# Two ways through the branch, gated sums by halves and a reordered second routing in a kernel of two transformer blocks

## What is computed

```python
def second_block(x, c, ...):
    cond = silu(c)
    for i in range(2):
        sh1, sc1, g1, sh2, sc2, g2 = split(cond @ ada_w[i] + ada_b[i], 6)
        h = modulate(rmsnorm(x, norm_g[i, 0]), sh1, sc1)
        y = mla_mixer(h, ...) if i == 0 else mamba2_mixer(h, ...)
        x = x + g1 * y
        h = modulate(rmsnorm(x, norm_g[i, 1]), sh2, sc2)
        y = swiglu(h, ...) if i == 0 else moe_swiglu(h, ...)
        x = x + g2 * y
    return rmsnorm(x, final_norm)

def moe_swiglu(h, w_router, w_gate, w_up, w_down):      # 8 experts, 2816 hidden features
    top_vals, top_idx = top_k(t @ w_router, 2)
    gates = sum(one_hot(top_idx, 8) * softmax(top_vals)[..., None], axis=1)
    for e in range(8):
        out = out + gates[:, e:e + 1] * swiglu(t, w_gate[e], w_up[e], w_down[e])
```

## Time and profile before

| | us |
|---|---|
| median of the runs | 2639.09 |
| profiled execution | 2639.72 |
| its span | 2638.0 |
| TensorE busy | 2205.1 (84%) |
| VectorE busy | 1437.7 (55%) |
| ScalarE busy | 1154.7 (44%) |
| GpSimd busy | 38.4 (1%) |
| DMA queue q1, share of the span | 66.9% |

### The profile page before, as it was taken

One profiled execution on the slowest core, in us unless ns is written; L12 is line 12 of the kernel. 1 busy time (PEld: TensorE's weight loads), 2 busy tenths in 40 slices (PEclk: granted clock), 3 DMA queues, 4 the chain that ended last, 5 costly groups with the idle time before them and its releaser, 6 DMA issues.

```text
span 2638.0 us, 29032 instructions
## 1 busy us (share of the span) xinstructions
PE 2205.1 (84%) x11922; PEld 1648.2 (62%) x11922; DVE 1437.7 (55%) x1992; ACT 1154.7 (44%) x1488; POOL 38.4 (1%) x107
## 2 busy tenths in 40 slices
PE   6888798766666665788899788877999999999997
PEld 6767566641122211456798677666887887878875
DVE  4744434442101100332554566655989988988997
ACT  3432334310000000242344356634777777777775
POOL 0000100000000000000000000000000000000000
PEclk9889898878777888897899889887999999999999
DMA  7441830329999999566345332143989989989994
GB/s 254 173 179 49 295 120 32 115 107 409 409 409 409 409 409 409 179 237 242 128 143 196 126 128 96 64 168 116 342 321 369 336 320 369 338 319 370 337 337 190
DMA packets 267673, 656.66 MB, mean 249 GB/s; under 512 B 13439, under 2 KB 38531, under 8 KB 267529
## 3 DMA queue, kind: packets, MB, share of 16 engines
q1 hardware_dynamic: 266576, 652.90, 66.9%
q10 hardware_dynamic: 952, 1.77, 0.2%
HBM read 653.60 MB, written 1.05 MB: 248 GB/s over the span
## 4 chain that ended last, share of the span: by engine, by line
PE 67%; DMA 16%; DVE 9%; ACT 5%; issue 2%; POOL 0%; ACTq 0%; DVEq 0%; POOLq 0%
PE psum L241 16%; PE psum L242 16%; PE psum L243 16%; PE psum L236 11%; DMA ring<-in_w_expert_up 5%; DMA ring<-in_w_expert_down 5%; DMA ring<-in_w_expert_gate 5%; PE psum L2257 2%; PE psum L1029 2%; PE psum L821 1%; DVE w_lo L186 1%; ACT w_hi L176 1%; PE psum L2279 1%; DMA ring<-in_ada_w 1%; PE psum L1975 1%
## 5 line engine op out<-in xcount | busy, mean ns | idle before, releaser
L186 DVE TENSOR_TENSOR w_lo<-ring,w_hi 128x1024 fp32r<-128x1024 f32 (+1 forms) x778 | 904.9, 1178 | 412.1 <-ACT w_hi L176 398.9
L176 ACT CAST w_hi<-ring 128x1024 fp32r<-128x1024 f32 (+1 forms) x778 | 785.1, 1015 | 437.7 <-PE psum L243 433.9
L241 PE MATMUL psum<-w_hi,xg_hi 128*128 128x512 f32 (+1 forms) x768 | 294.1, 383 | 1.2 <-ACT xg_lo L1947 1.2
L243 PE MATMUL psum<-w_lo,xg_hi 128*128 128x512 f32 (+1 forms) x768 | 289.1, 376 | 0.0
L242 PE MATMUL psum<-w_hi,xg_lo 128*128 128x512 f32 (+1 forms) x768 | 288.9, 376 | 0.0
L2257 PE MATMUL psum<-ring,hT 128*32 128x512 f32 x1024 | 166.4, 785 | 124.1 <-DMA ring<-in_w_expert_gate 63.7
L2257 PEld LDWEIGHTS psum<-ring,hT 128*32 128x32 f32 x1024 | 32.2, 128 | 252.8 <-DMA ring<-in_w_expert_up 92.4
L2116 DVE TENSOR_TENSOR x<-x,psum 128x1024 f32<-128x1024 f32 x16 | 19.5, 1222 | 267.5 <-PE psum L236 267.5
L241 PEld LDWEIGHTS psum<-w_hi,xg_hi 128*128 128x128 f32 x768 | 144.7, 188 | 30.4 <-issue 1.8
L242 PEld LDWEIGHTS psum<-w_hi,xg_lo 128*128 128x128 f32 x768 | 144.7, 188 | 29.0 <-issue 1.7
L243 PEld LDWEIGHTS psum<-w_lo,xg_hi 128*128 128x128 f32 x768 | 144.5, 188 | 28.5
(11 more groups left out here) (651 smaller groups left out, 3794.5 us busy)
## 6 DMA issues: line engine op xcount, KB each, us to landing
ring<-in_moe_w_gate SPq DMA_DIRECT2D x40, 2048.0 KB, 9.1
ring<-in_moe_w_up SPq DMA_DIRECT2D x40, 2048.0 KB, 10.0
ring<-in_moe_w_down SPq DMA_DIRECT2D x40, 2048.0 KB, 9.3
ring<-in_w_expert_gate SPq DMA_DIRECT2D x32, 2048.0 KB, 16.9
ring<-in_w_expert_up SPq DMA_DIRECT2D x32, 2048.0 KB, 17.1
ring<-in_w_expert_down SPq DMA_DIRECT2D x32, 2048.0 KB, 17.9
ring<-in_ada_w SPq DMA_DIRECT2D x24, 2048.0 KB, 8.2
ring<-in_ssm_w_in SPq DMA_DIRECT2D x10, 2048.0 KB, 7.9
```

The costliest lines, as they stand in the source:

```text
L176: a.copy(self.buffers(n, src.shape)[0], src).then_inc(*self.hi_made.up())
L186: v.tensor_tensor(lo, src, hi.bitcast(F32), SUB).then_inc(*self.lo_made.up())
L241: p.matmul(o, l[0], r[0], start=start, stop=False)
L243: return p.matmul(o, l[0], r[1], start=False, stop=stop)
```

## The change

- **By halves.** A new `by_halves_pe` takes all parts of a unit first, does half 0 of the columns for all of them, signals `half`, and then does half 1, signalling each part as used. The last units of ffn's down product and of ssm_out use it. VectorE adds half 0 after `half` and half 1 after the last part.
- **Low parts.** Behind the gated sums go the last low parts of the next stage: one of four in mla, two in ffn (of the first parts of ssm) and two in ssm_out. The first of them stands behind the norm's mean, the second of a pair behind VectorE's scaling (`beside`).
- **Branch of moe1.** VectorE's last two scatter sums move into both ways of the branch: ahead of the surplus cases, or in the `Else`, as `scatter_alone`.
- **Second routing.** The table moves behind expert 0's `selg`; the Exp goes ahead of the two row copies, with a first Exp on constants, right behind the scaling; the memset of `total` waits for hT.
- **Output.** Each tile of 128 tokens is stored by a DMA of its own.

```diff
+    def by_halves_pe(p, u, h, outs, done, first, kt, k_first=0):
+
+        parts = [split.take(p, n) for n in range(split.first[u], split.end(u))]
+        for half, out_ in enumerate(outs):
+            for n, (hi, lo) in enumerate(parts):
+                for t in range(NT):
+                    w = out_[t].shape[-1]
+                    ins = split_product(p, out_[t], tiles(h, first + n - k_first, slice(t * P, (t + 1) * P)),
+                                        tuple(b[:, 0, half * w:half * w + w] for b in (hi, lo)), first + n == 0, first + n == kt - 1)
+                if half:
+                    ins.then_inc(*split.used.up())
+            if not half:
+                ins.then_inc(*done.up("half"))
...
             v.tensor_scalar(M.selg[:, t, :], slots, M.pos[:, t, bass.ds(e, 1)], M.gate[:, t, bass.ds(e, 1)],
                             ALU.is_equal, MUL).then_inc(*d.up("selg", i))
+        after_selection()
...
-            expert_dve(v, run, i, i, slots, after_gate)
+            expert_dve(v, run, i, i, slots, after_gate, nothing if i else lambda: table_dve(v, run.st, run.moe))
...
         count = e.value_load(M.tab[0:1, 0:1], min_val=0, max_val=M.most_over)
         with e.If(count > 0):
+            if first:
+                first()
             finished(e, run.st)
...
         with e.Else():
-            e.nop()
+            if alone:
+                alone()
+            else:
+                e.nop()
...
-        scatter_dve(v, run1, last)
-        over_dve(v, run1, over1)
+
+        def scatter_alone():
+            for t in range(NT):
+                v.wait_ge(*S["moe1"].pe.of("scattered", last, t))
+                v.wait_ge(*S["moe1"].dve.of("acc", last - 1, t))
+                v.tensor_tensor(x[:, t, :], x[:, t, :], banks.of("moe1", "scatter", last, t), ADD).then_inc(S["moe1"].dve.sem, 1)
+
+        over_dve(v, run1, over1, lambda: scatter_dve(v, run1, last), scatter_alone)
...
-            split.make_lo(v, min(split.end(u) + PARTS, cap))
+            split.make_lo(v, split.end(u) + PARTS - half)
...
-            by_token_pe(p, unit["ff", 2, c], mid_ff, outs, first=4 * c, kt=22)
+            if c < len(ff_chunks) - 1:
+                by_token_pe(p, unit["ff", 2, c], mid_ff, outs, first=4 * c, kt=22)
+            else:
+                by_halves_pe(p, unit["ff", 2, c], mid_ff, outs, st.pe, 4 * c, 22)
...
         norm_mean_dve(v, st, xn_ff, ss_ff)
+        split.make_lo(v, split.first[unit["ff", 0, 0]] + PARTS)
         norm_dve(v, st, xn_ff, ss_ff, modulated_gain(1), modulated_shift(1), h_ff)
...
-        for c in range(len(ff_chunks)):
-            split.make_lo(v, min(split.end(unit["ff", 2, c]) + PARTS, cap))
-        v.wait_ge(*split.multiplied(unit["ff", 2, len(ff_chunks) - 1]))
+        last = unit["ff", 2, len(ff_chunks) - 1]
+        for c in range(len(ff_chunks) - 1):
+            split.make_lo(v, split.end(unit["ff", 2, c]) + PARTS)
         for half in range(2):
+            if half:
+                v.wait_ge(*split.multiplied(last))
+            else:
+                v.wait_ge(*st.pe.of("half"))
             gated_add(v, st, half, 1, halves_of(banks.of("ff_down", half)), sil_ff[:, :, 0:512]).then_inc(*d.up("x"))
...
-        norm_dve(v, st, xn_ssm, ss_ssm, modulated_gain(0), modulated_shift(0), h_ssm)
+        split.make_lo(v, split.first[b] + 3)
+        norm_dve(v, st, xn_ssm, ss_ssm, modulated_gain(0), modulated_shift(0), h_ssm,
+                 beside=lambda: split.make_lo(v, split.first[b] + 4))
...
-            by_token_pe(p, unit["ssm_out", n], zT_parts[n], outs, first=4 * n, kt=16, k_first=4 * n)
+            if n < 3:
+                by_token_pe(p, unit["ssm_out", n], zT_parts[n], outs, first=4 * n, kt=16, k_first=4 * n)
+            else:
+                by_halves_pe(p, unit["ssm_out", n], zT_parts[n], outs, st.pe, 4 * n, 16, k_first=4 * n)
...
-        split.make_lo(v, split_ends[1] + PARTS)
-        v.wait_ge(*split.multiplied(unit["ssm_out", 3]))
+        split.make_lo(v, split_ends[1])
         for half in range(2):
+            if half:
+                split.make_lo(v, split_ends[1] + 2)
+                v.wait_ge(*split.multiplied(unit["ssm_out", 3]))
+            else:
+                v.wait_ge(*st.pe.of("half"))
             gated_add(v, st, half, 0, halves_of(banks.of("ssm_out", half)), tmpy[:, :, :]).then_inc(*d.up("x"))
...
+        g.wait_ge(*S["moe2"].dve.of("hT", 4))
         g.memset(total[:, :, :], 0.0).then_inc(*S["moe2"].pool.up("total"))
...
         norm_rows_act(a, st, xn_moe, ss_moe)
+        a.activation(moe2.wts[:, :, 3:4], eps[:, 0:1].unsqueeze(1).to_broadcast([P, NT, 1]), ACT.Exp).then_inc(*st.act.up())
         a.wait_ge(*st.pe.of("logits"))
...
+        gates_act(a, st, moe2)
         for t in range(NT):
             a.wait_ge(*st.pe.of("rows", t))
             a.copy(h_rows[0][:, t, :], banks.of("rows", t)).then_inc(*st.act.up("rows", t))
-        gates_act(a, st, moe2)
...
-        norm_dve(v, st, xn_moe, ss_moe, modulated_gain(1), modulated_shift(1), None)
+        split.make_lo(v, split_ends[1] + 3)
+        norm_dve(v, st, xn_moe, ss_moe, modulated_gain(1), modulated_shift(1), None,
+                 beside=lambda: split.make_lo(v, split_ends[1] + 4))
...
         places_dve(v, st, moe2, rows_lo_dve)
-        table_dve(v, st, moe2)
...
-            v.scalar_tensor_tensor(total[:, t, :], x[:, t, :], fs[:, t:t + 1], fg, MUL, MUL).then_inc(*d.up("out"))
+            v.scalar_tensor_tensor(total[:, t, :], x[:, t, :], fs[:, t:t + 1], fg, MUL, MUL).then_inc(*d.up("out", t))
...
-        s.wait_ge(*S["last"].dve.of("out"))
-        s.dma_start(out[0].rearrange("(t p) n -> p t n", p=P), total[:, :, :]).then_inc(*stored.up(by=16))
+        for t in range(NT):
+            s.wait_ge(*S["last"].dve.of("out", t))
+            s.dma_start(out[0].rearrange("(t p) n -> t p n", p=P)[t], total[:, t, :]).then_inc(*stored.up(by=16))
```

More of the change, by code:

```diff
@@ L2127, in mid_dve, with expert_dve @@
         run.banks.empty(st.dve, st.name, "mid", i, ch)
-    def expert_dve(v, run, i, e, slots, after_gate):
+    def expert_dve(v, run, i, e, slots, after_gate, after_selection=lambda: None):
         M, st = run.moe, run.st
@@ L2212, in over_act, with over_dve @@
             expert_act(a, over, k, nothing)
-    def over_dve(v, run, over):
-        for k, e, b in over_cases(v, run, over):
+    def over_dve(v, run, over, first=None, alone=None):
+        for k, e, b in over_cases(v, run, over, first, alone):
             slots = run.moe.beyond[:, bass.ds(b, 1), :].rearrange("p a c -> p (a c)")
@@ L2220, in over_dve, with over_cases @@
             scatter_dve(v, over, k)
-    def over_cases(e, run, over):
+    def over_cases(e, run, over, first=None, alone=None):
         M = run.moe
```

## The result

The changed kernel takes 2621.13 us, the median of five runs (2619.4 to 2633.1), against 2639.09, also of five (2637.88 to 2644.76): 0.9925 of the time before, with a 95% interval of 0.9907 to 0.9942. The forecast was 2613.0, with a range of 2609 to 2619. It was faster, as forecast, but 18.0 us were gained and not 26.1. A second series on another chip gave 2621.69 (2616.22 to 2623.81), 0.9916 (0.9897 to 0.9934) of 2644.75 there.

The account below looks back on a forecast made before the run. TensorE was taken to set the pace in the expert stage, with serial passages between stages where it mostly waits. Gains there summed to 26.0 us, from the median 2639.09 to 2613.0 us; eight-in-ten range 2609 to 2619.

Parts of the forecast that it names:

- Moe1's branch, 5.37: Moe1 to mla: with the last two scatter sums behind VectorE's branch, mla's norm starts 5.37 us sooner.
- The rival "clock": After changed pauses, TensorE's clock level at stage starts can turn: -4 to +3 us; full gain at three starts, chance 0.05.
- Mla's low part, 2.2: Mla to ffn: one low part moved behind the gated sum lets the sum begin 2.22 us sooner, cost 0.
- Ffn, 4.7: Ffn to ssm: halves bring the norm 4.73 us sooner; 0.05 taken off for moved low parts, gain 4.7 us.
- TensorE's and ScalarE's branches, 0: Moe1's end: these engines keep their branches where they are; cost at most 0.4 us, taken as 0.
- Ssm_out, 4.73 - 2.4: Ssm_out to moe2: halves gain 4.73 us, a new TensorE wait for the fourth part costs 2.4; net 2.3.
- Memset, 1.1: Moe2's second routing: moving the memset of `total` behind hT stops it slowing VectorE's scaling, gain 1.1 us.
- Exp and table, 9.1: Moe2's second routing: Exp ahead of the row copies gains 4.4 us, the table behind the selections 4.7.
- Output, 1.25: Tail: storing the output in two DMAs lets the first half leave earlier, gain 1.25 us, between 0 and 1.4.
- Given back in the expert stage: Rival: a DMA stream paces TensorE in the expert stage, so moe2's 12.5 us are lost: 2625.5; chance 0.07.
- the fetch stays: Rival: mla's norm stands behind a second stall after the branch's join, so 5.37 us fall away: 2618.4; chance 0.10.
- no stall: Rival: ssm_out's four-part unit has no stall because buffers come free earlier than read: 2610.6; chance 0.05.

Follow-up runs that it names:

- the changed kernel's repeat: The changed kernel as it is, measured and profiled once more on another chip: 2621.69 us.

## Why the prediction was wrong, point by point

- **Moe1's branch, 5.37.** That the pause goes, and its size, hold: 5.4 alone, 5.6 in the changed kernel's repeat (3.9 in its first profile). What fills the pause is argued and not shown: in the trace of before three packets of the instruction queues move between 1068 and 1072 us, inside it, which agrees with a fetch of code. The step that failed is what stands behind it: "Gain 5.37 us" was booked as the kernel's gain. Alone the branch is worth 5.4 - 4.0 = 1.4 by these two stages, 0.1 from moe1's norm to the end, and 0.9990 by the runs.
- **The rival "clock".** It had the right mechanism, and I sized it from the starts of mla, ffn and ssm at 1.5 us each, with the sentence "Most of that is in my range", and gave a chance only to the good side. Mla loses 4.0 us by it, and most of it not at its start but between 90 and 130 us into the stage. Its +3 end, 2616, was inside the range; the real 4.0 with the next point was not.
- **Mla's low part, 2.2.** Exact alone (198.4). "The moved low part (1.23 us) falls into VectorE's wait for the rstd, 1.21 us. Cost 0": this step failed too. The wait was GpSimd's work, and the low part held GpSimd up: 0.84 us in ffn, 0.95 in ssm, 0.60 in moe2, 2.4 together, where the prediction had 0 and 0.05.
- **Ffn, 4.7.** The end of the stage is as forecast, 2.69 us from the second half's product to the norm. The stage gained 4.1 to 4.2; with the low parts behind the scaling 4.7 (204.9), the term that the prediction gave.
- **TensorE's and ScalarE's branches, 0.** They cost nothing in the changed kernel. TensorE's could be seen only where it was given work behind: that began 3.5 us behind its last product. The branch is what stands between in its program; no run takes it out.
- **Ssm_out, 4.73 - 2.4.** Pause 2.48, at the place and with the releaser named. Its removal brought 2.7 in the passage and 2.6 in the medians. The halves themselves are worth 4.66 (18.65 to 13.99 us from the last unit's first product to the norm, without the pause). Over the two profiles of each kernel the stage's mean gained nothing, 2.4 less than forecast; 0.95 of that is GpSimd's, 0.7 the mean loss to the half clock behind the pause (in one profile of two), and 0.4 the pause's cost of 2.7 and not 2.4; 0.3 is open.
- **Memset, 1.1.** Scaling in 0.75 us as forecast, but 0.6 later for GpSimd's sake: 0.5 net on the transposes, and 1.1 with the low parts behind the scaling.
- **Exp and table, 9.1.** Right within a tenth (854.5 to 845.5 alone).
- **Output, 1.25.** 1.3 (9.5 to 8.2).
- **Given back in the expert stage; the fetch stays; no stall.** None came true. Nor the slower case: the clock in the expert stage was 1.00.

Added up: 26.0 less 4.0 (clock in mla) less 2.4 (GpSimd) is 19.6, or 2619.5: these two, put at 0 and 0.05 in the sum, are enough to take the time out of the range. The medians gave 18.0 and 23.1, and the mean lengths of the two profiles of each kernel from moe1's norm on give 19.1 (2092.3 to 2073.2). What is left lies in stages that aren't the same twice, moe1 (0.6 less than forecast) and ssm above all, and is open.

## What to carry to other kernels

A pause that is taken out ahead of TensorE isn't worth its length until the granted clock of what follows has been looked at: here 5.4 us became 1.4, and 14 products of a constant in the next pause brought mla's 4.0 back, and 1.4 more. On the kernel before the same products brought mla nothing, so a filling has to be measured where it is put. "It fits into that engine's wait" is half of the question; the other half is which engine it waits for, and whether the moved work holds that one up. And a helper that takes all its inputs first is worth a look for the one place where there are as many inputs as buffers.

## What the runs showed of the hardware that I had not expected

- A GpSimd instruction of 0.22 us took 1.05, one of 0.71 took 1.74, when a subtraction of two SBUF tensors ran on VectorE (1.22 us).
- The clock of TensorE went to half behind 3.73 us of busy time on products of 32 columns (0.99, then 0.58), with pauses of no more than 1.05 us ahead of them.
- A shorter pause (5.2 and not 10.5 us) left the products behind it colder, not warmer: 10 in the first 4 us, not 12.
- With the branch over `over_cases` between them, TensorE's constants began 3.52 us behind its last scatter product, and the timeline gives only "issue" for the time in between.
